# First norm and first projection slots of a two-block transformer kernel: products with a diagonal in place of scaled rows

## The reference

```python
def rmsnorm(x, w):
    xf = x.astype(jnp.float32)
    y = xf * lax.rsqrt(jnp.mean(xf * xf, axis=-1, keepdims=True) + EPS)
    return (y * w.astype(jnp.float32)).astype(x.dtype)
...
        h = rmsnorm(x, norm_w[layer])
        proj = h @ w_in[layer]
        (u_pool, g_pool, q, kc_raw, vc_raw, k_sel, v_sel, k_win, v_win,
         g_nsa, g_br) = jnp.split(proj, split_at, axis=-1)
```

## Time and profile before

| | us |
|---|---|
| median of 3 runs | 2862.84 |
| lowest, highest | 2862.38, 2863.79 |
| the profiled execution | 2863.12 |
| its span, first to last instruction | 2860.5 |
| TensorE busy | 2822.6 (99%) |
| VectorE busy | 1849.4 (65%) |
| ScalarE busy | 1255.6 (44%) |
| GpSimd busy | 697.7 (24%) |

### The profile page before, as it was taken

How to read it: one execution, slowest core, us unless ns; L and a number is a source line. 1 busy time by engine, 2 the same in 40 slices (tenths; PEclk the granted TensorE clock), 3 DMA queues, 4 the chain that set the end, 5 groups by cost and what they waited for, 6 DMA issues and landing times.

```text
span 2860.5 us, 40415 instructions
## 1 busy us (share of the span) xinstructions
PE 2822.6 (99%) x15369; PEld 2452.3 (86%) x15369; DVE 1849.4 (65%) x2501; ACT 1255.6 (44%) x1399; POOL 697.7 (24%) x450
## 2 busy tenths in 40 slices
PE   8999999999999999999999999999999999999998
PEld 7888888998988889878888888888888888888886
DVE  5557767665665666775799996565565555555555
ACT  4336544544345444544444444333334444444444
POOL 0000025222000000000288878888840000000000
PEclk9999999999999999999999999999999999999999
DMA  5557544566555554344567777666666666666665
GB/s 211 195 197 249 208 162 171 196 215 235 200 178 190 188 205 153 147 141 176 184 193 216 213 214 213 194 185 189 190 202 239 238 239 240 236 219 218 216 214 189
DMA packets 153041, 576.21 MB, mean 201 GB/s; under 512 B 50672, under 2 KB 83568, under 8 KB 90224
## 3 DMA queue, kind: packets, MB, share of 16 engines
q1 hardware_dynamic: 70992, 513.95, 51.6%
q10 hardware_dynamic: 38944, 44.06, 4.5%
q0 software_dynamic: 43008, 16.93, 3.6%
HBM read 547.47 MB, written 27.39 MB: 201 GB/s over the span
## 4 chain that ended last, share of the span: by engine, by line
PE 96%; DVE 2%; ACT 1%; issue 0%; DMA 0%; ACTq 0%; SPq 0%; DVEq 0%
PE bank L523 34%; PE bank L1042 24%; PE bank L528 18%; PE bank L568 11%; PE bank L790 2%; PE bank L509 2%; PE bank L728 1%; DVE wlo L1778 1%; PE bank L637 1%; PE bank L813 1%; PE bank L713 0%; PE bank L618 0%; PE bank L486 0%; PE bank L699 0%; PE bank L700 0%
## 5 line engine op out<-in xcount | busy, mean ns | idle before, releaser
L1778 DVE TENSOR_TENSOR wlo<-raw,whi 128x2048 fp32r<-128x2048 f32 (+1 forms) x484 | 1104.2, 2282 | 779.7 <-ACT whi L1077 778.9
L1077 ACT ACTIVATE whi<-raw 128x2048 fp32r<-128x2048 f32 (+1 forms) x484 | 921.9, 1905 | 1321.6 <-PE bank L523 689.6
L523 PE MATMUL bank<-hT,whi 128*128 128x512 f32 x4272 | 1043.8, 393 | 0.0
L523 PEld LDWEIGHTS bank<-hT,whi 128*128 128x128 f32 x4272 | 781.6, 188 | 147.6 <-DVE hT L2047 0.9
L1732 POOL DMA_INDIRECT gates_dram<-R x256 | 580.8, 2269 | 795.8 <-DVE R L2549 678.8
L528 PEld LDWEIGHTS bank<-hT,wlo 128*128 128x128 f32 x4272 | 547.4, 191 | 22.6 <-DVE wlo L1778 1.7
L528 PE MATMUL bank<-hT,wlo 128*128 128x256 f32 x4272 | 554.0, 283 | 1.2 <-DVE wlo L1778 1.2
L1042 PE MATMUL bank<-whi,ghi 128*128 128x512 f32 x1016 | 271.7, 389 | 0.2 <-issue 0.2
L1042 PE MATMUL bank<-wlo,ghi 128*128 128x512 f32 x1016 | 271.5, 389 | 0.0
L1042 PE MATMUL bank<-whi,glo 128*128 128x512 f32 x1016 | 271.5, 389 | 0.0
L568 PE MATMUL bank<-whi,hT 128*128 128x512 f32 x1016 | 244.5, 393 | 2.1 <-ACT whi L1077 0.9
(11 more groups left out here) (353 smaller groups left out, 1977.1 us busy)
## 6 DMA issues: line engine op xcount, KB each, us to landing
raw<-stream SPq DMA_DIRECT2D x484, 1024.0 KB, 4.8
gates_dram<-token_scale POOLq DMA_DIRECT2D x128, 128.0 KB, 4.6
R<-gates_dram ACTq DMA_DIRECT2D x128, 128.0 KB, 3.9
R<-cmpw ACTq DMA_DIRECT2D x16, 512.0 KB, 4.7
acts_dram<-R ACTq DMA_DIRECT2D x32, 256.0 KB, 5.5
R<-acts_dram ACTq DMA_DIRECT2D x64, 128.0 KB, 3.8
gates_dram<-R POOLq DMA_INDIRECT x256
xres<-x SPq DMA_DIRECT2D x2, 1024.0 KB, 6.1
```

Source lines behind the costliest of these rows:

```text
L523: return mm(bank[to][:], whi[t][:, k * P:(k + 1) * P], hT2[:, k, :, :].rearrange("p a t -> p (a t)"), start=(at == 0), stop=(at == KC - 1))
L1077: A(whi[t][:, 0:w], raw[t][:, 0:w], ACT.Copy).then_inc(hi_ready[t], 1)
L1778: V.tensor_tensor(wlo[t][:, 0:w], raw[t][:, 0:w], whi[t][:, 0:w].bitcast(F32), ALU.subtract).then_inc(raw_free[t], 1)
```

## The change

Four edits, all at the start (n = 0):

1. Squares are shared: ScalarE sums the squares of columns 0 to 1023 of each block, VectorE those of columns 1024 to 2047 by a `tensor_tensor_reduce`, and adds the two sums.
2. x is no longer scaled. VectorE multiplies the identity by the reciprocal roots, one 128 x 128 diagonal for each block, and TensorE forms `xres` piece (stationary) times diagonal, which turns and scales at once. `turn_piece(0, f)` issues the same number of matmuls as before.
3. `hTh` of turn piece 0 is made by VectorE; ScalarE makes those of pieces 1 to 7. `hTh_part` is therefore one lower in all later phases, and the waits of `low_parts` with it.
4. `first_two("in_t", 0)`, until now used for the other norms, takes the place of `turn_piece` 6 and 7 and of the first two slots: 12 `both` of slot 0, turn pieces 6 and 7, 12 `both` of slot 1, then the rest of slot 0 and of slot 1.

```diff
@@ turn_piece (PE)
-                elif f % 4 == 0:
-                    pe.wait_ge(xn_ready, 2 * n + f // 2 + 2)
+                elif n == 0 and f == 0:
+                    for b in range(TB):
+                        pe.wait_ge(x_block[b], 16)
+                    pe.wait_ge(first_diagonal, 1)
+                elif n == 2 and f % 4 == 0:
+                    pe.wait_ge(xn_ready, f // 2 + 2)
...
-                    rows_ = xres[:, b, k * P:(k + 1) * P] if n % 2 else scr_of[n][:, b * D + k * P:b * D + (k + 1) * P]
-                    last = nc.tensor.transpose(turn_bank(n, f)[:, c * P:(c + 1) * P], rows_, ident)
+                    to = turn_bank(n, f)[:, c * P:(c + 1) * P]
+                    if n == 0:
+                        last = mm(to, xres[:, b, k * P:(k + 1) * P], diagonal[:, b, :], start=True, stop=True)
+                    elif n == 2:
+                        last = nc.tensor.transpose(to, scr_of[2][:, b * D + k * P:b * D + (k + 1) * P], ident)
+                    else:
+                        last = nc.tensor.transpose(to, xres[:, b, k * P:(k + 1) * P], ident)
...
@@ start of the PE program (first_two itself is moved up unchanged)
-            turn_norm(0)
-            phase_t2("in_t", 0)
+            for f in range(6):
+                turn_piece(0, f)
+            first_two("in_t", 0)
+            for s in range(2, RING):
+                t2_slot("in_t", 0, s)
+            with pe.Fori(1, G0["in_t"][1]) as i:
+                for s in range(RING):
+                    t2_slot("in_t", i, s)
...
@@ start of the ACT program
-                A(scr_of[0][:, b * D:(b + 1) * D], xres[:, b, :], ACT.Square, accum_out=ssq[:, b:b + 1]).then_inc(sq_done, 1)
+                A(scr_of[0][:, b * D:b * D + 1024], xres[:, b, 0:1024], ACT.Square, accum_out=ssq[:, b:b + 1]).then_inc(sq_done, 1)
...
-            high_parts(0, "norm1")
+            high_parts(0, "norm1", range(1, 8))
@@ low_parts (DVE)
-                    dve.wait_ge(hTh_part, 8 * n + f + 1)
+                    if (n, f) != (0, 0):
+                        dve.wait_ge(hTh_part, 8 * n + f)
...
@@ start of the DVE program
-            dve.wait_ge(sq_done, 2)
-            mean_square(0)
             for b in range(TB):
                 dve.wait_ge(x_block[b], 16)
-            scaled(0, lambda b: xres[:, b, :], rstd)
+                half = xres[:, b, 1024:D]
+                last = V.tensor_tensor_reduce(scr_of[0][:, b * D + 1024:(b + 1) * D], half, half, 1.0, 0.0, ALU.mult, ALU.add,
+                                              sums2[:, b:b + 1])
+            step(last)
+            dve.wait_ge(sq_done, 2)
+            step(V.tensor_tensor(ssq, ssq, sums2[:, 0:2], ALU.add))
+            mean_square(0)
             dve.wait_ge(few_params, 16)
+            for b in range(TB):
+                last = V.tensor_scalar(diagonal[:, b, :], ident, rstd[:, b:b + 1], None, ALU.mult)
+            last.then_inc(first_diagonal, 1)
+            dve.wait_ge(turned, 1)
+            for k in range(2):
+                last = V.tensor_scalar(hTh[:, k, :], turn_bank(0, 0)[:, k * T:(k + 1) * T], column("norm1", k), None, ALU.mult)
+            step(last)
             low_parts(0, "norm1")
```

More of the change, by code:

```diff
@@ L379, in build_two_blocks @@
         branch_high, branch_split = sem("branch_high"), sem("branch_split")
+        first_diagonal = sem("first_diagonal")
         y_high, y_split, half_merged = sem("y_high"), sem("y_split"), sem("half_merged")
@@ L484, in turn_piece @@
                     k, b = 2 * f + c // 2, c % 2
-                    rows_ = xres[:, b, k * P:(k + 1) * P] if n % 2 else scr_of[n][:, b * D + k * P:b * D + (k + 1) * P]
-                    last = nc.tensor.transpose(turn_bank(n, f)[:, c * P:(c + 1) * P], rows_, ident)
-                last.then_inc(turned, 1)
[L489 to L496, removed]
+                    to = turn_bank(n, f)[:, c * P:(c + 1) * P]
[5 more added lines that the diff above has]
+                        last = nc.tensor.transpose(to, xres[:, b, k * P:(k + 1) * P], ident)
+                last.then_inc(turned, 1)
             def t_slot(name, i, s, between=None, order=range(KC), ready=None):
@@ L541, in t2_slot, with first_two, both @@
                 last.then_inc(slot_used[t], 1)
[L543 to L549, removed]
+            def first_two(name, n):
+                def both(s, k):
+                    return mm(bank[s][:], whi[s][:, k * P:(k + 1) * P], hT2[:, k, :, :].rearrange("p a t -> p (a t)"),
+                              start=(k == 0), stop=(k == KC - 1))
+                for s in range(2):
+                    pe.wait_ge(bank_free[s], B0[name][s])
+                    pe.wait_ge(hi_ready[s], rounded(name, 0, s))
+                    for k in range(3 * KC // 4):
+                        if s == 0 and k % 2 == 0:
+                            pe.wait_ge(hTl_part, 8 * n + k // 2 + 1)
+                        both(s, k)
+                    if s == 0:
+                        turn_piece(n, 6)
+                        turn_piece(n, 7)
+                for s in range(2):
+                    for k in range(3 * KC // 4, KC - 1):
+                        if s == 0 and k % 2 == 0:
+                            pe.wait_ge(hTl_part, 8 * n + k // 2 + 1)
+                        both(s, k)
+                    pe.wait_ge(raw_free[s], consumed(name, 0, s))
+                    for k in range(KC):
+                        mm(bank[s][:, 0:T], wlo[s][:, k * P:(k + 1) * P], hTh[:, k, :], start=False, stop=False)
+                    both(s, KC - 1).then_inc(slot_used[s], 1)
             def phase_t(name, lo=0, hi=None, between=None):
@@ L808, in _ @@
                 n_slots("out1", i, out1_ready)
[L810 to L834, removed]
             def turn_scale(n, to):
```

## The result

The changed kernel takes 2868.22 us (median of 20 runs, 2865.75 to 2869.38), the kernel before 2862.72 (20 runs, 2862.17 to 2863.95): a ratio of 1.0018, 95% interval 1.0012 to 1.0024. It is **5.5 us slower**, just under the 0.2% that the prediction took as the least that a measurement can tell, and clear of no change with 20 runs; the forecast was 2862.8 with a range to 2864.8. The profiled execution of the changed kernel took 2867.75 us, its span 2865.9, 5.4 more than before.

The account below looks back on a forecast made before the run. TensorE, busy 99% of the span, was taken as the bound, so only the start of slot 2 counted: -1.56 us at the start, +1.5 given back, net -0.06, forecast 2862.8 us, range 2861.2 to 2864.8.

Parts of the forecast that it names:

- part 1: Way to the first matmul: with shared squares and diagonals it comes 1.56 us earlier than 12.59, at 11.03.
- first rival: Squares at the start: VectorE's reduction takes 2.29 us at half pace, slot 2 at about 32.1, total 2863.8; chance 0.13.
- Part 3: Turn pieces 6 and 7 behind the twelfth `both`: ScalarE and VectorE run dry, taking back 2.3 us of VectorE's time.
- Part 4: TensorE up to slot 2: idle 3.1 us until 22.6, then no wait; slot 2 starts at 31.1, 0.06 earlier.
- second rival: TensorE's gap from 19.5 to 22.6: the clock falls to 1.2 GHz, losing 1.7 us, total 2864.5; chance 0.12.

Follow-up runs that it names:

- one_pass_filler: The changed kernel with transposes in place of the products with the diagonal (scaling left out) and 22 idle transposes in TensorE's gap: 2864.14 us.
- filler: The changed kernel with 22 transposes of the identity, which nothing reads, behind turn piece 7 where TensorE stood idle: 2865.85 us.
- old_order: The changed kernel with the order of before on TensorE: all eight turn pieces first, then slots 0 and 1 one after the other: 2864.10 us.
- order_alone_filler: The kernel before with only the first two slots interleaved (turn pieces 6 and 7 behind the twelfth `both`), plus 22 idle transposes in the gap: 2866.11 us.
- squares_alone: The kernel before with only the squares of columns 1024 to 2047 moved to VectorE: 2862.44 us.
- changed_again: The changed kernel itself, measured again beside the kernel before: 2868.38 us, 5.7 over before.

## Why the prediction was wrong

**The failing step is in part 1: "A true product with a diagonal costs what a transpose does."** All records of the two lines, in the changed kernel and in the kernel before:

```profile
L492 PE MATMUL bank<-R,xres x64: 270/275/550, 10.8 to 22.9; 128*128 128x128 f32 x64
```

```profile
L486 PE MATMUL bank<-par,R x64: 272/273/447, 12.6 to 1257.6; 128*128 128x128 f32 x64
```

Each record lasts as long, 275 against 273 ns, and so I had compared durations. But L492 has 64 records for the 32 products of one norm, L486 64 for the 64 transposes of two norms. The evidence stood in the earlier trace rows: L840 has 8 records, and the program has 4 such products (two calls of two). I read the duration and not the count. In the sum that step doubled TensorE's work up to piece 5, 48 records, at the slow pace of the first 4.7 us: `low_parts` 5 ended at 20.45 instead of 18.0, and all that hangs on it came 2.4 later. one_pass_filler against filler measures it: 2.45 us at slot 2, 2.4 by the spans. This step alone does not make the 5.5 us; the new order with its half clock, below, cost more: 4.1 us, by old_order.

**Part 1 otherwise** held. The reduction took 1226 ns with a read of 83 (I took 1.22 + 0.08), and the first matmul came at 10.84 for 11.03, with x landed 0.25 earlier in that execution. The first rival, half-pace squares, is out: 1226 ns for two float32 operands from SBUF is full pace. The Trainium skill (Vector Engine (DVE) Microarchitecture Reference, Points that are easy to get wrong) states its rule of half throughput for one form of instruction, `S2S2D2_STT`; I took the squares for such a case, and for this instruction the rule does not hold: the measurement decides. Whether `tensor_tensor_reduce` has that form no run shows.

**Part 3, the pause,** held in kind and nearly in size: 2.3 us taken back on VectorE was forecast; its wait was 2.13 in one_pass_filler and 2.75 in the changed kernel. It also released the raw tile of slot 0 late, as argued, and that load did hold slot 2 in one_pass_filler, where it came 0.5 later than forecast. In the changed kernel TensorE's own backlog held it. What the pause costs at slot 2 was put too low: 1.4 to 1.5 without the gain of the start, 2.4 in order_alone_filler.

**Part 4** saw a gap of 3.1 us; it was 2.82. But the forecast let TensorE come out of it at full clock. **The second failing step is this term, put at nothing, and the second rival happened** at its place: priced at 1.7, the slow 15 `both` measured 1.5 us in the one profile and 2.8 in the other, and filling the gap took 2.4 to 2.6 off the medians. Against it I had argued that the gap is shorter than the stretch at 1240 and that products precede it. That was weak, since the earlier trace rows hold only one gap that kept the clock, of 1.23 us, and nothing between 1.23 and the stretch at 1240.

**The range** was wrong in its form too: each rival was added to the forecast alone, and the upper end, 2864.8, was the dearest of them. One rival came together with a cost that none of them had, as the two do not exclude each other. At slot 2 of the profiled execution the account closes: 31.1 as forecast, 0.48 more in one_pass_filler with its later load, 2.45 from there to filler for the products, 1.47 for the clock and 0.47 for the longer slow pace at the start make 35.97. Of the 5.4 us of its span about 0.6 is left, which I can place but not prove: in the profiled executions the slow clock around 1250 lasts 10.2 us in the changed kernel and 3.4 in before. That is no mark of the change alone: squares_alone, which is no slower than before, has the long one too, and changed_again the short one. one_pass_filler has the long one as well, which may be why its span is 0.8 over before with 0.4 at slot 2. No run isolated that stretch; both stay open.

## What to carry to other kernels

Count an operation's records against the instructions that the program issues before taking its duration as its price: a float32 product was two records here, a transpose one. Where work is interleaved to fill a wait, look at which producer's input now stands behind it in TensorE's queue: pieces that other engines need come first, filler last. And an idle stretch of some 3 us on a full TensorE can cost more than its length, since the backlog behind it may run at half clock; price rivals that can occur together as a sum.

## What the runs showed of the hardware

- Float32 products of 128 x 128 x 128 appear as two records each, 0.11 us apart at full clock (16 records in 1.80 us); transposes of the same size as one, at the same distance (8 in 1.03 us). A product so takes TensorE twice as long.
- TensorE's slow pace at the start ended at another time in each execution: 48 records of the same program took 7.83, 7.35 and 7.19 us in the changed kernel, changed_again and filler.
- Idle stretches of 2.82 and 3.11 us came with a granted clock of 0.50 for 3.4 to 6.8 us; with 22 transposes in them, leaving 0.4 to 0.7 us idle, it stayed at 1.00 in all three kernels tried, as it did around a gap of 1.23 us before. Transposes of the identity that nothing reads suffice.
- A raw tile's load took 4.8 us when issued at 23.5 (before), 5.7 when issued at 25.8 (order_alone_filler) and 6.2 when issued at 24.5 (old_order), each with the next one 2.2 behind it. What makes the difference stays open.
